# Memory keys and values of a two-layer block, made between the masked attention units instead of after the output projection

## What is computed

```
x = x + 0.5 * swiglu(norm(x), ffn1)
h = norm(x)                       # mixers on h @ w_mix_in
o = concat(norm(MLA(h)),          # 8 heads, 512 x 512 scores, no mask
           norm(SWA(h)),          # 4 heads, window 128, bias and sink   } masked
           norm(NA(h)))           # 4 heads, 8x16 neighbourhood, bias    } units
x = x + o @ w_mix_out
m = norm(mem) * mem_norm_m        # mem: 256 memory tokens
k, v = norm(m @ w_k), m @ w_v     # 4 heads of 64: keys and values
q = norm(norm(x) @ w_q)           # needs the x of the line above
x = x + softmax(q k^T / 8) v @ w_o
x = x + 0.5 * swiglu(norm(x), ffn2);  x = norm(x)
```

## Time and profile before

| what | value |
|---|---|
| three timed runs | 2985.71, 2981.44 and 2985.39 us, median 2985.39 |
| profiled execution, its own time | 2981.31 us |
| its span in the profile | 2979.5 us |
| granted clock of TensorE, mean | 0.988 |
| PE busy | 2887.5 us, 97% of the span |
| DVE, ACT, POOL busy | 1453.0, 1097.5, 223.8 us |

### The profile page before, as it was taken

One profiled execution on the slowest core, in us unless ns is written; L12 is line 12 of the kernel. 1 busy time (PEld: TensorE's weight loads), 2 busy tenths in 40 slices (PEclk: granted clock), 3 DMA queues, 4 the chain that ended last, 5 costly groups with the idle time before them and its releaser, 6 DMA issues.

```text
span 2979.5 us, 36258 instructions
## 1 busy us (share of the span) xinstructions
PE 2887.5 (97%) x13458; PEld 2315.7 (78%) x13458; DVE 1453.0 (49%) x2090; ACT 1097.5 (37%) x1784; POOL 223.8 (8%) x166
## 2 busy tenths in 40 slices
PE   8999999899999999998999999999999999999998
PEld 5698777688788886677878888888886677788886
DVE  5673476534444434555454443544334655454432
ACT  4512343343323223655432222323224655432221
POOL 0000000000100022000120003000121001110011
PEclk9999999999999999999999999999999999999999
DMA  3101211024222323010222232222322111122232
GB/s 121 67 22 47 85 64 57 15 95 131 92 96 94 105 92 110 29 57 23 85 81 95 99 108 90 88 95 99 104 94 84 41 50 43 64 96 94 99 107 77
DMA packets 68363, 238.06 MB, mean 80 GB/s; under 512 B 10272, under 2 KB 12448, under 8 KB 67616
## 3 DMA queue, kind: packets, MB, share of 16 engines
q1 hardware_dynamic: 66240, 227.87, 23.0%
q10 hardware_dynamic: 2016, 8.77, 0.8%
HBM read 234.51 MB, written 2.10 MB: 79 GB/s over the span
## 4 chain that ended last, share of the span: by engine, by line
PE 68%; DVE 3%; ACT 2%; issue 1%; DVEq 0%; ACTq 0%
PE bank L381 19%; PE bank L383 19%; PE bank L382 19%; PE bank L860 3%; PE bank L886 3%; PE bank L665 2%; PE bank L872 2%; PE bank L638 1%; ACT L_probs L930 1%; DVE L_scores L978 1%; PE bank L1512 0%; PE bank L227 0%; PE bank L1455 0%; DVE L_area L1821 0%; ACT L_h_hi L1642 0%
## 5 line engine op out<-in xcount | busy, mean ns | idle before, releaser
L381 PE MATMUL bank<-L_h_hi,L_w_hi 128*128 128x512 f32 x1776 | 703.5, 396 | 6.1 <-DVE residual L1831 3.8
L382 PE MATMUL bank<-L_h_lo,L_w_hi 128*128 128x512 f32 x1776 | 692.5, 390 | 0.0
L383 PE MATMUL bank<-L_h_hi,L_weight_ring_low 128*128 128x512 f32 x1760 | 685.9, 390 | 0.0
L369 ACT CAST L_w_hi<-L_weight_ring 128x1024 fp32r<-128x1024 f32 (+2 forms) x290 | 324.1, 1118 | 910.2 <-PE bank L383 899.9
L375 DVE TENSOR_TENSOR L_weight_ring_low<-L_weight_ring,L_w_hi 128x1024 fp32r<-128x1024 f32 (+2 forms) x290 | 393.0, 1356 | 376.9 <-ACT L_w_hi L369 376.8
L381 PEld LDWEIGHTS bank<-L_h_hi,L_w_hi 128*128 128x128 f32 x1776 | 334.2, 188 | 82.5 <-issue 5.7
L382 PEld LDWEIGHTS bank<-L_h_lo,L_w_hi 128*128 128x128 f32 x1776 | 334.1, 188 | 74.7 <-issue 5.7
L383 PEld LDWEIGHTS bank<-L_h_hi,L_weight_ring_low 128*128 128x128 f32 x1760 | 330.8, 188 | 69.1
L381 PE MATMUL bank<-L_act_hi,L_w_hi 128*128 128x512 f32 x704 | 273.9, 389 | 0.0
L382 PE MATMUL bank<-L_act_lo,L_w_hi 128*128 128x512 f32 x704 | 273.9, 389 | 0.0
L383 PE MATMUL bank<-L_act_hi,L_weight_ring_low 128*128 128x512 f32 x704 | 273.9, 389 | 0.0
(11 more groups left out here) (329 smaller groups left out, 3884.0 us busy)
## 6 DMA issues: line engine op xcount, KB each, us to landing
L_weight_ring<-ffn_in SPq DMA_DIRECT2D x174, 512.0 KB, 3.2
L_weight_ring<-ffn_out SPq DMA_DIRECT2D x64, 704.0 KB, 4.0
B_weight_ring<-w_sqk SPq DMA_DIRECT2D x24, 512.0 KB, 3.3
B_weight_ring<-w_dn SPq DMA_DIRECT2D x16, 512.0 KB, 3.3
B_weight_ring<-w_gate SPq DMA_DIRECT2D x16, 512.0 KB, 3.2
L_weight_ring<-w_sna_qk SPq DMA_DIRECT2D x16, 512.0 KB, 3.3
L_weight_ring<-w_mix_out SPq DMA_DIRECT2D x16, 512.0 KB, 3.2
B_weight_ring<-w_sv SPq DMA_DIRECT2D x12, 512.0 KB, 3.3
```

The costliest lines, as they stand in the source:

```text
L369: e.copy(hv.high(at)[:, 0:width], hv.raw(sh, at)[:, 0:width]).then_inc(hv.w_hi_done, 1)
L381: e.matmul(out, a_hi, b_hi, start=start, stop=False)
L382: e.matmul(out, a_hi, b_lo, start=False, stop=False)
L383: return e.matmul(out, a_lo, b_hi, start=False, stop=stop)
```

## The change

The norm of the memory, its values and its two key tiles move from behind the output projection to the steps between the masked units. Their sums use a part of bank 0. The normalised memory moves to other places on chip (parts of `v_mla`, of the rotary table `cs2`, and a new tile `memory_rows`). The strips of w_mem_v and of the memory keys now come ahead of the eight output strips in the ring. So the first two output strips are loaded later, and their two splits move from beside the last two jobs to between units 58 and 59 and between units 60 and 61 (the steps numbered by the unit whose maximum and exponential they make). The key jobs carry "rest": each is cut in a step that finishes the job before and a step that multiplies. The second key job waits until the first is done. After the output projection only the two query jobs remain; their matmuls wait tile by tile for the halves of x. In `mem_turns` the split of w_mem_o now stands behind the first unit step. The core of the diff:

```diff
+            for i in range(2):
+                mix_jobs.append(dict(pair, parts=k_parts(1, KT, P, m_n, NMEM), width=NMEM, gain=g("memk"), skip=2 - 2 * i,
+                                     needs=(jb.done, jobs_before + 25) if i else (v_done, (layer + 1) * (2 * TT + 2)),
+                                     sum_at=(0, NMEM), sum_needs=(jb.gained, jobs_before + 25 + i), rest=True,
+                                     dest=(qk[:, 2 * i + 1, :], P)))
+            mem_jobs[0]["each"] = (sh.h_done, layer * H_PER + 2 * KT)
...
-            mix_turns += ["unit"] + ["split"] * (i >= 10) + ["unit"] + {18: ["norm_used"]}.get(i, []) + ["job"]
-        mix_turns += ["unit", "unit", "row"] * 4
-        mix_turns += ["unit"] * 4 + ["norm", "unit"] * 3 + ["norm", "unit", "norm_used", "unit", "unit", "row"]
-        mix_turns += ["unit"] * 2 + ["row"] + ["unit"] * 4
+            mix_turns += ["unit"] + ["split"] * (10 <= i < 18) + ["unit"] + {18: ["norm_used"]}.get(i, []) + ["job"]
+        mix_turns += ["mem_norm", "unit", "unit", "row", "mem_rows", "unit", "mem_rows", "unit", "row"]
+        mix_turns += ["mem_v", "unit", "mem_v", "unit", "row", "mem_v", "unit", "mem_v", "unit", "row"]
+        mix_turns += ["unit", "job", "unit", "unit", "job", "unit"]
+        mix_turns += ["job", "norm", "unit", "norm", "unit", "job", "norm", "unit", "norm", "unit"]
+        mix_turns += ["norm_used", "unit", "split", "unit", "row", "unit", "split", "unit", "row"] + ["unit"] * 4
...
-        mem_turns = ["job"] * 4 + ["unit"] * 3 + ["job"] + ["unit"] * (4 * TT - 2)
-        mem_turns[2:2] = ["split"]
+        mem_turns = ["job", "x_norm", "job", "unit", "split", "unit", "unit", "job"] + ["unit"] * (4 * TT - 2)
...
-                    at = resid_sp(e, seen, sh, at, lambda n, part: A["w_mix_out"][layer, n], 1)
                     for i in range(2):
                         at = load_strip(e, seen, sh, at, A["w_mem_v"][layer, i])
-                    for i in range(4):
+                    for i in range(2):
+                        at = load_strip(e, seen, sh, at, A["w_mem_qk"][layer, i])
+                    at = resid_sp(e, seen, sh, at, lambda n, part: A["w_mix_out"][layer, n], 1)
+                    for i in range(2, 4):
                         at = load_strip(e, seen, sh, at, A["w_mem_qk"][layer, i])
...
+                    def memory_values_pe():
+                        w = [strip_here(e, seen, sh, at0 + sna_at + 8 + i) for i in range(2)]
+                        for t in range(NMEM // P):
+                            for i in range(2):
+                                if t == 0:
+                                    e.wait_ge(m_done, layer * KT + 4 * i + 4)
+                                for k in range(KT // 2):
+                                    mm = e.matmul(banks[0][:, t * NMEM:(t + 1) * NMEM], m_n[i * 4 + k][:, t * P:(t + 1) * P],
+                                                  w[i][:, k * NMEM:(k + 1) * NMEM], start=(i == 0 and k == 0),
+                                                  stop=(i == 1 and k == 3))
+                                if t == NMEM // P - 1:
+                                    mm.then_inc(sh.strip_done, 1)
+                                yield
...
+                    def memory_norm_act():
+                        norm_act(e, seen, sh, NMEM, bank=0)
+                        yield
+
+                    def memory_values_act():
+                        for _ in range(3):
+                            yield
+                        e.wait_ge(sh.strip_done, seen.ready(sh.strip_done, 2))
+                        for t in range(2):
+                            e.copy(v_mem[:, t, :], banks[0][:, t * NMEM:(t + 1) * NMEM]).then_inc(v_done, 1)
+                        yield
...
+                    def memory_rows_dve():
+                        e.wait_ge(sh.rstd_done, seen.ready(sh.rstd_done))
+                        for k in range(KT):
+                            e.scalar_tensor_tensor(out=m_n[k], in0=memT[:, k, :], scalar=g("memm")[:, k:k + 1],
+                                                   in1=sh.rstd[:, 0:NMEM], op0=ALU.mult, op1=ALU.mult)\
+                                .then_inc(m_done, 1)
+                            if k in (3, 7):
+                                yield
...
-                    norm_act(e, seen, sh, NMEM, rstd=lat_rstd)
                     for n in range(KT):
                         e.wait_ge(sh.strip_done, seen.ready(sh.strip_done))
-                        if n < KT - 2:
+                        if n < KT - 1:
                             split_strip_act(e, seen, sh, hv, at0 + mix_out_at + n + 2, KT * P)
...
-                    e.wait_ge(turned, 10 * layer + KT)
-                    e.wait_ge(sh.rstd_done, seen.ready(sh.rstd_done))
-                    for k in range(KT):
-                        e.scalar_tensor_tensor(out=m_n[:, k, :], in0=memT[:, k, :], scalar=g("memm")[:, k:k + 1],
-                                               in1=lat_rstd[:, 0:NMEM], op0=ALU.mult, op1=ALU.mult)\
-                            .then_inc(m_done, 1)
```

More of the change, by code:

```diff
@@ L221, in norm_pool, with norm_pe @@
             also(k)
-def norm_pe(e, seen, sh, width=T):
+def norm_pe(e, seen, sh, width=T, bank=7):
     e.wait_ge(sh.sq_summed, seen.ready(sh.sq_summed))
-    e.matmul(sh.banks[7][:, 0:width], sh.ones[:, :], sh.sq_sum[:, 0:width], start=True,
+    e.matmul(sh.banks[bank][:, 0:width], sh.ones[:, :], sh.sq_sum[:, 0:width], start=True,
              stop=True).then_inc(sh.norm_mm, 1)
@@ L637, in finish @@
         e.wait_ge(jb.rstd, seen.free(jb.rstd) + fewer)
-        e.matmul(banks[sum_banks[b % len(sum_banks)]][:, 0:width], ones[0:kn, :], jb.sq[0:kn, b, 0:width], start=True,
+        if "sum_needs" in job:
+            e.wait_ge(*job["sum_needs"])
+        e.matmul(job_sum(banks, sum_banks, job, b), ones[0:kn, :], jb.sq[0:kn, b, 0:width], start=True,
                  stop=True).then_inc(jb.summed, 1)
@@ L643, in jobs_pe_steps @@
             finish(j - 1)
+        if j < len(jobs) and "rest" in jobs[j]:
+            yield
         if j < len(jobs):
@@ L1139, in layers_program @@
         v_mla = area(TT, 512)
+        m_n = [v_mla[:, 1 + k // 2, k % 2 * NMEM:(k % 2 + 1) * NMEM] for k in range(4)] + \
+            [x[:, k * NMEM:(k + 1) * NMEM] for x in (cs2, memory_rows) for k in range(2)]
+        v_mem = v_mla[:, 3, :].rearrange("p (t d) -> p t d", t=2)
         cq = area(2, T)
@@ L1235, in plan @@
                                      number=jobs_before + 1 + len(mix_jobs)))
[L1236 to L1241, removed]
+            for i in range(2):
[3 more added lines that the diff above has]
+                                     dest=(qk[:, 2 * i + 1, :], P)))
+            mem_jobs = [q_job(i, scaled_qg[:, layer, 3:4], mem_parts, number=jobs_before + len(mix_jobs) + 1 + i) for i in range(2)]
+            mem_jobs[0]["each"] = (sh.h_done, layer * H_PER + 2 * KT)
             for job in mix_jobs[5:]:
@@ L1504, in _, with x_norm_pe @@
                     at += KT
[L1506 to L1513, removed]
-                                              stop=(i == 1 and k == 3))
-                        mm.then_inc(sh.strip_done, 1)
-                    norm_pe(e, seen, sh)
-                    seen.ready(v_done, 2)
+                    def x_norm_pe():
+                        norm_pe(e, seen, sh)
+                        yield
                     seen.ready(sh.h_done, KT)
                     take_turns(mem_turns, job=jobs_pe_steps(e, seen, sh, jb, at, mem_jobs, hv, True, mem_first, inside=mem_first),
-                               unit=attn_pe_steps(e, seen, sh, at_, mem_units, ident))
-                    at += 4
+                               unit=attn_pe_steps(e, seen, sh, at_, mem_units, ident), x_norm=x_norm_pe())
+                    at += 2
                     e.wait_ge(at_.o_done, 2 + 10 * layer + 10)
@@ L1653, in _ @@
                                                               pause=True),
-                               unit=attn_act_steps(e, seen, sh, at_, mix_units), norm=norms, row=rows, split=splits_act())
+                               unit=attn_act_steps(e, seen, sh, at_, mix_units), norm=norms, row=rows, split=splits_act(),
+                               mem_norm=memory_norm_act(), mem_v=memory_values_act())
                     for t in range(TT):
@@ L1813, in _ @@
                                unit=attn_dve_steps(e, seen, sh, at_, mix_units, stores("mix", o_tok, 8)),
-                               norm_used=scales, row=rows, split=splits_dve())
+                               norm_used=scales, row=rows, split=splits_dve(), mem_rows=memory_rows_dve(),
+                               mem_v=memory_values_dve())
                     next(scales)
```

76 lines of the change are left out of this document (49 added, 27 removed).

## The result

The changed kernel takes 2991.67 us (median of 7 runs, 2990.24 to 2996.11), the kernel before 2984.39 in the same comparison (7 runs); the ratio is 1.0029, with an interval of [1.002, 1.0039]. It is slower by 0.3%, and the interval leaves out 1. Forecast were 2995.4 and a loss of 10 us; measured are a loss of 7.3 and a time inside the range of the forecast's own case.

The account below looks back on a forecast made before the run. PE, busy 97%, bounds the kernel; between units without other matmuls the chain of scores, maximum, exponential and transposes does. Six parts sum to +5.0 us a layer, +10 in two: 2985.4 + 10 = 2995.4 us, range 2975 to 3003.

Parts of the forecast that it names:

- the forecast's own case: Whole kernel: slower by 10 us, 2995.4 us, own range 2990 to 3001; chance 0.45.
- Part 1: Output projection's end to first memory scores: values and keys leave, 0.6 us wait at first query's sum; -13.7 us a layer.
- Parts 2 and 3: Masked unit steps: moved matmuls +14.6, idle filled less new waits -2.2, extra ACT work +0.8 us a layer.
- part 3: Second twelve unit steps: ACT gets Ln and Exp of the second key tile; +0.8 us a layer.
- Part 4: Units 58 to 61: two output splits lengthen the exponential chain by 2.6 each, PE without reserve; +5.0 us a layer.
- Part 5: Output strip 2: DVE's memory rows no longer ahead of its split, PE starts sooner; -1.9 us a layer.
- Part 6: First memory units: w_mem_o split behind the first step delays the third unit's maximum by 2.7; +2.4 us a layer.
- A: Rival: splits slip into ACT's idle time, moved matmuls fill all idle of the unit steps; 2972.6 to 2977.4 us, chance 0.20.
- B: Rival, a wash: output splits and w_mem_o split cost half; +2.4 us over two layers, 2987.8 us, chance 0.23.
- C: Rival: new waits make the clock fall twice more a layer, 1.7 us each; +7 on the forecast, 3002 us, chance 0.12.

Follow-up runs that it names:

- kernel 1: Changed kernel with the two output-strip splits ahead of the two memory key jobs instead of between units 58 to 61; 2977.56 us, ratio to before 0.9988.
- kernel 6: Kernel before with DVE's eight memory rows behind the first two residuals instead of ahead of output strip 2's split; 2980.62 us, ratio 0.9979.
- Kernel 2: Changed kernel with the w_mem_o split ahead of the norm of x instead of behind the first memory unit step; 2990.37 us, ratio to before 1.0023.
- kernel 5: kernel 3 with DVE's two halves of the w_mem_o split behind the first query's scaling instead of ahead of it; 2976.55 us, ratio to before 0.9968.
- kernel 3: Changed kernel with both edits, those of kernel 1 and Kernel 2; 2975.58 us, ratio to before 0.9975.

## Why the prediction was right, step by step

*Part 1*, -13.7 forecast: the way from the projection's end to the first memory scores fell from 27.53 to 13.68, -13.85, and the wait at the first query's sum is 0.55 for 0.6.

*Parts 2 and 3*, +14.6 - 2.2 + 0.8 = +13.2: kernel 1 shows them without the splits, 12.66 and 12.24 us more than before. The terms were off both ways. PE's busy time of layer 0's two stretches rose by 15.2 (34.27 + 18.09 - 20.11 - 17.04), for 14.6. The idle time of the first stretch fell by 2.66 (4.27 to 1.61), for 2.2; that of the second rose by 0.13 (1.11 to 1.24), so the 0.8 of part 3 isn't there. Of the new waits the first value matmul has 0.56 (0.5 forecast), the second key tile 0.67 (1.2). The prediction has all of PE's waits among the masked units of the kernel before go to exponentials; one more, 0.4 us, was for ACT's copy.

*Part 4*, +5.0: 5.06 between the changed kernel and kernel 1 up to unit 62. The mechanism was right with the size: the chain of exponentials grew by 2.49 and 2.73 (2.6 each forecast), and PE had no reserve. What I expected to see of it on PE was not: PE's transposes waited 1.17 and 1.07 us behind the splits, not 1.5 to 2, because matmuls at the lower clock filled the rest of the time. That fall of the clock my sum left out. It cost nothing inside the steps and 1.0 us in each layer behind them, up to strip 2.

*Part 5*, -1.9: the wait went from 1.89 to 0.29, so 1.6 went, and kernel 6 has -1.61 for this edit alone. In the changed kernel 1.06 and 1.11 are left of it, because of that clock. The lower clock behind the old wait, which I named and left out, went too: 34.38 us of projection became 32.77 in layer 0.

*Part 6*, +2.4: 11.47 against 9.05, +2.42; the third unit's maximum comes 5.86 us behind the first scores, for 3.12 before, 2.74 later (2.7 forecast; the earlier trace rows have the old place). Kernel 2 takes the loss away. The third unit's maximum in the changed kernel, behind the two low halves:

```profile
1475.23 2.36 DVE L375 TENSOR_TENSOR L_weight_ring_low<-L_weight_ring,L_mix_rounded 128x1024 fp32r<-128x1024 f32 x2 [1.96 <-ACT L_mix_rounded L369]
1477.51 0.75 DVE L1015 TENSOR_REDUCE L_neg_max<-bank 128x1 f32<-128x256 f32 x2
```

The sum of a layer was +5.0; the table has +3.6 and +3.1. In layer 0 the difference is the projection's clock (-1.6) and the way to unit 62 (+17.7 for +18.2), against 0.8 that part 5 fell short by. In layer 1 it is +17.3 for +18.2, the same 0.8, and the way to w_mem_o, 18.62 to 16.99, which the runs show to come and go with no edit near it. The falls of the clock, left out of the sum, came at one place and went at others; that they nearly cancel is luck.

*The rivals.* A's condition, exponentials of units 58 and 59 within 1.3 us, failed in the changed kernel (3.47) and holds in kernel 1 (0.98). With the w_mem_o split moved as well, kernel 5 is in A's range and kernel 3 just outside it (0.9968 and 0.9975 of before; A gave 0.9957 to 0.9973). Less of that is due to the interleaving than A supposed: kernel 6, which interleaves nothing, is at 0.9979, kernel 5 at 0.9968, and their intervals overlap. From the last job's sum to the fifth memory unit kernel 6 takes 125.39 and 125.86 us, kernel 5 123.65 and 123.68: what kernel 5 has beyond kernel 6, above all the matmuls among the units, is worth 1.7 and 2.2 us a layer. The rule of the Trainium skill on which A leaned, page Perfetto Trace Analysis, section Optimization Strategy (interleaving may help where the most contended engine changes), agrees with that gain; the changed kernel shows it lost to the splits that changed place with the rest. B fails on part 4, where its half price was 2.4. C's mechanism was there, the clock falling at the new waits, but it cost 1.0 us a layer on top of part 4 and not 3.4, and an old fall, that behind strip 2 in layer 0, went.

## What to carry to other kernels

Matmuls moved into the waits of a chain over three engines do fill them, but count also what the moved work had been covering: here four strip splits lost their cover, and cost 5 us (the two among the last units, with another 1.0 through the lower clock behind them) and 2.4 us (the two of w_mem_o) a layer, more than the filled idle time gave. Place what ACT and DVE must do between two steps of such a chain under a block of matmuls or in the other engine's latency, where the same instructions cost 0.15 us or nothing that the trace shows. And try the cheapest part of a large change alone first: eight DVE instructions placed later gave 0.21% of the 0.32% that the best version reached, though the two intervals overlap.

## What the hardware showed that I had not expected

The clock fell without a long idle time. In the changed kernel PE waited 1.17, 1.07 and 1.27 us within 9 us with matmuls between, and the mean granted clock of that stretch was 0.91, part of it at the lower level of 1.2 GHz; in kernel 1, with one wait of 0.99 there, it was 1.00, 2.4 GHz throughout. The matmuls right behind the first of the three waits are slow already. The Trainium skill, page TensorE: Matmul & The Clock Gate, section A second HAM failure mode: psum-queue depth-cycling, tells of a bf16 kernel in which small idles between groups of matmuls made the clock swing between its levels; the rows of the changed kernel agree. Such waits don't always bring it down: in the kernel before, with five of up to 1.1 us in the masked units, the first stretch ran at 1.00 in layer 0 and at 0.93 in layer 1.

The same stretch may also run at either level in one execution. In kernel 5 the way from the fifth memory unit to w_mem_o took 16.98 us in layer 0 and 18.63 in layer 1, with the same matmuls:

```profile
1473.45:1490.43 16.98, 14.19 (x104) 12.85 (x105) 7.41 (x19) 12.43 (x39) 0.00 (x0) 0.99 0.01 1
2567.94:2586.57 18.63, 15.84 (x104) 14.31 (x104) 7.41 (x19) 12.76 (x39) 0.00 (x0) 0.89 0.00 1
```

Over the eight kernels six of sixteen such stretches are at the short value, the rest at the long one, with no edit that explains which. The 48 matmuls with w_mem_o behind them vary as well, from 11.29 to 15.00 us. A gain of 1.6 us read at one place of one execution can be this and nothing else.
